# Experts of a mixture-of-experts layer in 13 blocks of mixed pieces instead of 14 of equal ones, a second fixed block, and gathers without empty rows

## What is computed

```python
def _hier_moe(h, w_group, b_group, w_expert, b_expert, w1, w3, w2):
    ...
    g_sel = jnp.argmax(g_logits, axis=-1)
    ...
    top_v, top_i = lax.top_k(e_in, MOE_TOPK)
    gate = (p_g * jax.nn.softmax(top_v, axis=-1)).reshape(-1)
    ids = (g_sel[:, None] * MOE_EXPERTS_PER_GROUP + top_i).reshape(-1)
    ...
        return (jax.nn.silu(xr @ w1[e]) * (xr @ w3[e])) @ w2[e]
```

## Time and profile before

| | |
|---|---|
| median of 3 runs | 2820.74 us |
| the profiled execution | 2825.79 us |
| its span, first to last instruction | 2823.7 us |
| TensorE, VectorE, ScalarE, GpSimd busy | 92%, 56%, 23%, 6% of the span |
| DMA, bytes moved | 618.46 MB, of which expert weights 384 x 1024 KB |
| chain that ended last, by engine | TensorE 12%, DMA 4%, SyncE's queue 1% of the span (as far as it was followed back) |

### The profile page before, as it was taken

One profiled execution on the slowest core, in us unless ns is written; L12 is line 12 of the kernel. 1 busy time (PEld: TensorE's weight loads), 2 busy tenths in 40 slices (PEclk: granted clock), 3 DMA queues, 4 the chain that ended last, 5 costly groups with the idle time before them and its releaser, 6 DMA issues. The chain is left out here.

```text
span 2823.7 us, 34710 instructions
## 1 busy us (share of the span) xinstructions
PE 2608.0 (92%) x12926; PEld 1701.4 (60%) x12926; DVE 1587.3 (56%) x3139; ACT 650.0 (23%) x1415; POOL 158.5 (6%) x179
## 2 busy tenths in 40 slices
PE   6999899999999999979788799999799898899998
PEld 4888788999468888858645233333487544233332
DVE  4887577777578888767534143334544723233334
ACT  4122365565311110012232100000213512000000
POOL 0000222322000000000100000000000000000000
PEclk8999899999999999989999899999999999999999
DMA  8321311110645537623045999999422049999998
GB/s 310 134 83 60 106 35 42 31 33 14 264 146 179 175 131 239 215 99 142 16 180 242 419 419 419 419 420 419 179 83 75 1 198 383 420 419 419 419 419 356
DMA packets 114129, 618.46 MB, mean 219 GB/s; under 512 B 13136, under 2 KB 13728, under 8 KB 64160
## 3 DMA queue, kind: packets, MB, share of 16 engines
q1 hardware_dynamic: 103680, 581.39, 52.3%
q0 software_dynamic: 8832, 30.44, 3.2%
q10 hardware_dynamic: 1440, 4.29, 0.4%
HBM read 606.51 MB, written 9.56 MB: 218 GB/s over the span
## 5 line engine op out<-in xcount | busy, mean ns | idle before, releaser
L3274 PE MATMUL bank<-arena 128*32 128x512 f32 (+2 forms) x2048 | 404.6, 607 | 32.2 <-DMA arena<-in_w 19.4
L530 PE MATMUL bank<-arena 128*128 128x256 f32 x1776 | 414.0, 387 | 21.5 <-ACT arena L498 13.7
L530 PEld LDWEIGHTS bank<-arena 128*128 128x128 f32 x1776 | 340.5, 193 | 92.5 <-issue 34.6
L3274 PEld LDWEIGHTS bank<-arena 128*32 128x32 f32 (+2 forms) x2048 | 133.9, 131 | 277.8 <-issue 266.9
L3302 PE MATMUL bank<-arena 128*32 128x512 f32 (+2 forms) x1024 | 211.7, 640 | 36.8 <-DMA arena<-in_w 34.5
L3316 PE MATMUL bank<-arena 128*128 128x512 f32 x448 | 219.7, 614 | 5.4 <-DVE arena L3437 1.8
L266 PE MATMUL bank<-arena 128*128 128x512 f32 (+1 forms) x608 | 211.6, 503 | 0.9 <-PEq L2713 0.9
L3451 DVE SCALAR_TENSOR_TENSOR arena<-bank,arena 128x512 f32<-128x512 f32 x224 | 168.3, 751 | 73.6 <-PE bank L3316 61.6
L3302 PEld LDWEIGHTS bank<-arena 128*32 128x32 f32 (+2 forms) x1024 | 70.0, 137 | 173.7 <-issue 169.4
L266 PEld LDWEIGHTS bank<-arena 128*128 128x128 f32 x608 | 114.5, 189 | 94.3 <-issue 87.3
L3316 PEld LDWEIGHTS bank<-arena 128*128 128x128 f32 x448 | 71.4, 188 | 151.5 <-DVE arena L3451 90.0
(11 more groups left out here) (500 smaller groups left out, 3900.3 us busy)
## 6 DMA issues: line engine op xcount, KB each, us to landing
arena<-in_w SPq DMA_DIRECT2D x384, 1024.0 KB, 24.7
arena<-in_dense SPq DMA_DIRECT2D x180, 512.0 KB, 4.5
arena<-in_mods SPq DMA_DIRECT2D x128, 512.0 KB, 4.7
arena<-core_rows POOLq DMA_DIRECT2D x48, 256.0 KB, 3.8
arena<-in_xT SPq DMA_DIRECT2D x2, 2048.0 KB, 11.0
token_rows<-arena ACTq DMA_DIRECT2D x8, 512.0 KB, 2.6
arena<-c_row_silu SPq DMA_DIRECT2D x5, 512.0 KB, 4.6
gdn_gate<-arena POOLq DMA_DIRECT2D x8, 256.0 KB, 2.7
```

Source lines behind the costliest of these rows:

```text
L530: mm = pe.matmul(out, w[:, k, :], x[:, k, :], start=(k == 0), stop=(k == K1 - 1))
L3274: mm = pe.matmul(self.bank[2 + t][part, :], xT[i % 2][:, 2 * q + k, part], w[j][:, k, t, :], start=(q == 0 and k == 0), stop=(q == 3 and k ...
```

## The change

The blocks are cut anew: `KINDS` is `ffmmtwttmmmmm`, 13 blocks. `f` is now two blocks, with the experts 28 to 31 (64 rows each); `w` one block of 128; `t` has 96 + 32 rows; `m` 64 + 32 + 32. A lane of 96 rows is two pieces, 64 and 32 columns, with the same weights. The first fixed block is still made by matmuls; the second is gathered, but its experts are known, so SyncE loads its weights ahead of the wait for the order. In layer 1 the early loads are 15 instead of 12; load 15 waits for the transposed norm factor, whose buffer shares its place. A slot without a pair now gets the number 4096, and the gathers leave out rows with numbers over 511; GpSimd clears the two row buffers first. The routing's formulas for a rank's first slot and for its number of rows are new. The spare blocks become 18, still not run.

```diff
-KINDS = "fqpwpqwpwqwppq"
-FIXED = 2
-LANES = {"f": FIXED, "w": 1, "p": 2, "q": 4}
+KINDS = "ffmmtwttmmmmm"
+LANES = {"f": (64, 64), "w": (128,), "t": (96, 32), "m": (64, 32, 32)}
+FIRST_FIXED = NE - FIXED
...
-MOE_EARLY = [12, 12]
+MOE_EARLY = [12, 15]
...
+def pieces_of(kind):
+    at, pieces = 0, []
+    for j, lanes in enumerate(LANES[kind]):
+        while lanes:
+            n = 1 << (lanes.bit_length() - 1)
+            lanes -= n
+            pieces.append((j, slice(at, at + n), lanes == 0))
+            at += n
+    return pieces
...
-            dve.tensor_copy(self.slot_tok, toks).then_inc(s["slots"], 1)
+            dve.tensor_scalar(self.slot_tok, toks, float(NO_ROW), None, ALU.add).then_inc(s["slots"], 1)
...
+                    if n == MOE_RING - 1:
+                        sp.wait_ge(self.rstd_turned, 1)
                     if n >= MOE_RING:
                         sp.wait_ge(s["used"], n - MOE_RING + 1)
...
+                    if i == FIXED_BLOCKS:
                         self.clear_past(sp)
                         sp.wait_ge(self.order_ready, 1)
...
+                for i in range(2):
+                    last = pool.memset(xr[i], 0.0)
+                self.pool.after(pool, last)
                 pool.wait_ge(self.rows_stored, 64)
...
-                    pool.indirect_dma_start(xr[i % 2], None, self.rows[:, :],
-                                            bass.IndirectOffsetOnAxis(at, 0)).then_inc(x_in[i % 2], 16)
+                    pool.indirect_dma_start(xr[i % 2], None, self.rows[:, :], bass.IndirectOffsetOnAxis(at, 0),
+                                            bounds_check=L - 1, oob_is_err=False).then_inc(x_in[i % 2], 16)
...
                         for k in range(2):
                             for t in range(2):
-                                for j, part in enumerate(parts):
+                                for j, part, last in pieces:
                                     mm = pe.matmul(self.bank[2 + t][part, :], xT[i % 2][:, 2 * q + k, part], w[j][:, k, t, :],
                                                    start=(q == 0 and k == 0), stop=(q == 3 and k == 1))
-                                    if k == 1 and t == 1:
+                                    if k == 1 and t == 1 and last:
                                         mm.then_inc(s["used"], 1)
```

More of the change, by code:

```diff
@@ L33 @@
 NG, EG = 4, 8
-KINDS = "fqpwpqwpwqwppq"
-FIXED = 2
-LANES = {"f": FIXED, "w": 1, "p": 2, "q": 4}
-WIDE, PAIRS, QUADS = (KINDS.count(kind) for kind in "wpq")
-HALF, QUARTER = P // 2, P // 4
[L39 to L43, removed]
+KINDS = "ffmmtwttmmmmm"
+LANES = {"f": (64, 64), "w": (128,), "t": (96, 32), "m": (64, 32, 32)}
+COUNT = {kind: KINDS.count(kind) for kind in LANES}
+FIXED_BLOCKS = COUNT["f"]
+FIXED = FIXED_BLOCKS * len(LANES["f"])
+FIRST_FIXED = NE - FIXED
+HALF, QUARTER = P // 2, P // 4
+FIRST_THREE = FIXED + COUNT["w"]
+FIRST_HALF = FIRST_THREE + COUNT["t"]
+BESIDE_THREE = FIRST_HALF + COUNT["m"]
+THIRD = BESIDE_THREE + COUNT["t"]
+FOURTH = THIRD + COUNT["m"]
+assert FOURTH + COUNT["m"] == NE and COUNT["w"] == 1
+FIRST_BLOCK = {"f": 0, "w": FIXED_BLOCKS, "t": FIXED_BLOCKS + 1, "m": FIXED_BLOCKS + 1 + COUNT["t"]}
+MAIN = len(KINDS)
+OVF = 18
 BLOCKS = MAIN + OVF
@@ L128, in constant_tables @@
     e = np.arange(NE)
-    t["bonus"] = np.tile(2048.0 * np.maximum(FIXED - e, 0) - e / 64.0, (P, 1))
+    t["bonus"] = np.tile(2048.0 * np.where(e < FIRST_FIXED, 0, NE - e) - e / 64.0, (P, 1))
     t["fold"] = row % 64 == np.arange(36)[None, :]
@@ L3186, in experts_of @@
                 def experts_of(i):
-                    return list(range(FIXED)) if i == 0 else [expert(r) for r in seq[i][1]]
+                    return [FIRST_FIXED + r for r in seq[i][1]] if i < FIXED_BLOCKS else [expert(r) for r in seq[i][1]]
                 for i in range(N + 1):
@@ L3220, in _ @@
                     sp.wait_ge(s["added"], KD * N)
+                    if layer == 0:
+                        sp.wait_ge(ss, 1)
                     spare_sync(sp)
@@ L3260, in hidden @@
                 def hidden(i, quarters):
-                    parts = seq[i][2]
+                    ranks, pieces = seq[i][1:]
                     if quarters[0] == 0:
@@ L3297, in output @@
                     for t in halves:
-                        w = [slot_in(pe, first2[i] + t * len(parts) + j).rearrange("p (k n) -> p k n", k=4)
-                             for j in range(len(parts))]
+                        w = [slot_in(pe, first2[i] + t * len(ranks) + j).rearrange("p (k n) -> p k n", k=4)
+                             for j in range(len(ranks))]
                         for k in range(4):
-                            for j, part in enumerate(parts):
+                            for j, part, last in pieces:
                                 mm = pe.matmul(self.bank[7 - t][part, :], aT[:, k, part], w[j][:, k, :],
                                                start=(k == 0), stop=(k == 3))
-                                if k == 3:
+                                if k == 3 and last:
                                     mm.then_inc(s["used"], 1)
@@ L3552, in gpsimd_steps @@
         def gpsimd_steps(pool):
+            for i in range(2):
+                pool.memset(xr[i], 0.0).then_inc(cleared, 1)
+            pool.wait_ge(cleared, 2)
             for b in range(B):
```

87 lines of the change are left out of this document (50 added, 37 removed).

## The result

The changed kernel takes 3224.97 us, the median of 4 runs (3222.83 to 3227.96), against 2820.9 us of the kernel before on the same chip: a ratio of 1.1431, 95% interval 1.1413 to 1.1449. The forecast was 2813.3 us. What happened is the second rival, the one with a chance of 0.20: pieces of 64 and of 32 columns don't run at the same time.

The account below looks back on a forecast made before the run. Each layer was taken as bound by DMA bytes after the expert loads' restart, plus what follows the last landing. -2.0 - 5.8 - 5.5 + 3.8 + 2.1 = -7.4 us gave 2813.3 us (-0.26%), range 2801 to 2815, chance 0.47.

Parts of the forecast that it names:

- the second rival: Expert matmuls: 64- and 32-wide pieces don't run at the same time; 15.0 instead of 7.0 us a run, about 3157 us; chance 0.20.
- TensorE inside the stretch: Expert blocks while loads stream: 30.3 us of TensorE against 46.0 of transport if pieces run side by side; costed at nothing.
- Early loads: Expert loads 12 to 15 cross the idle 31 us before the restart; gain 1.0 us a layer, 2.0 in all.
- Gathers: Gathers behind load 28: empty rows left out save their full bytes, 9.8 ns each; -5.8 and -5.5 us.
- Tail: End of each layer: TensorE finishes later after the last landing, as the last block has three experts; +2.1 and +3.8 us.
- The first rival: Whole kernel: nothing measurable, through dearer width changes in the tail (2820.5 us) or empty rows costing as full (2822.1); chance 0.28.
- Costed at nothing: Routing and layer start: two more VectorE instructions (some 1.3 us), two GpSimd memsets and moved semaphore clears delay nothing.

Follow-up runs that it names:

- one-width kernel: The changed kernel with every piece of the ten t and m blocks cut to 32 columns: 2823.49 us, ratio 0.9998 against the kernel before.
- half runs: one-width kernel, each gather leaving out the half of its partitions that one bit names: 2819.5 us (bit 0), 2825.3 (bit 6), 2822.7 for the kernel before.
- edit of the tail: one-width kernel with half scatters done earlier in the last blocks: 2819.63 us, ratio 0.9987 against the kernel before.

## Why the prediction was wrong

**The step that failed.** The term "TensorE inside the stretch" was set to nothing on the condition "if the pieces run side by side". The prediction took it because the changes of width in the trace before are "all between pieces that share columns, so they bind no piece to others' columns". That argument says only that those rows can't show an exclusion; it was read as if they spoke against one. The runs show in its place that a 64 and a 32 on other columns take turns: a run of 15.88 instead of 7.0 us, and back to 7.0 with one width. The Trainium skill, TensorEngine Tiling (Array Packing), section Key Properties, has the rule: changing the tiling mode, and not only the tile, drains the array. By that rule the rival was the forecast, and the trace agrees, with 14.27 us for a run that changes four times and 15.88 for one that changes sixteen times.

**The rival's price.** It had 15.0 us a run and 3157 us in all, against 15.88 and 3225. It took eight pairs of changes at 0.15; a pair costs 0.26 (2.12 / 8). Thirty runs a layer at 0.88 are 26 of the 34 us a layer that it was short; the layer ended at 2205.8 instead of near 2175.

**Early loads.** As forecast in place: load 16 left at 1528.3 (1529 forecast), the 31 us carried 184 instead of 68 GB/s, and load 28 landed 6.5 us after its issue instead of 8.4, in layer 1 7.1 instead of 7.8. That is 1.9 and 0.6 us sooner where 1.0 and 1.0 stood, though with mixed pieces nothing waited for it; in the one-width kernel it was 1.6 and 0.1.

**Gathers: the second step that failed.** The software queue moved 24.74 MB, 5.7 MB less, as forecast. But "the DMA time follows bytes in every row I have, so I take the full saving" was wrong. Of 5.8 and 5.5 us the one-width kernel saved 4.4 in layer 0 (423.1 to 418.7) and lost 0.6 in layer 1 (422.0 to 422.6). In every row before, all partitions were fetched, so bytes and the fullest sixteenth went together; the half runs part them. The fullest group went from 80 rows in ten gathers to 72 in nine in layer 1 and to 68 in layer 0, which by the line above is worth 1.2 and 1.7 us, not 5.5 and 5.8. Runs that should be alike differ by up to 2 us in this measure, so layer 1 fits. That layer 0 saved more than its share stays open, since all three profiles of this layout show it.

**Tail.** The mechanism was right: +2.1 and +3.8 us were forecast, and the one-width kernel's last scatter ends 2.0 and 4.0 us later after the last landing than before. That the size fits so well is luck in part, since two errors cancel. The last block's first quarter started 38.8 us ahead of the last landing, not 37.6; and from there to the end of the first half's scatter TensorE took 42.7 and 43.0 us, not 41.4, because the first output half ran 5.08 and 5.34 us where the forecast had 3.65. The edit of the tail confirms the cause, since 3.1 us of each came back when TensorE's work behind the first quarter's loads was cut.

**The sum without the widths.** -7.4 was forecast, and the one-width kernel gave -0.02% (-0.11% to +0.07%), so 2 us slower to 3 us faster. The gathers in layer 1, 6.1 us short, account for most of the gap. The first rival, no measurable difference, would have been right for this kernel, and by a mechanism that it named, empty rows that cost as much as full ones, though only in layer 1.

**Costed at nothing.** The memsets (1.84 us on GpSimd in the 31 us) and the routing's new instructions delayed nothing: the second fixed block starts at 1560.69, where the quad block started at 1561.59.

## What to carry over

Pieces of a packed matmul should have one column width per stretch of work; in these fp32 runs two widths on disjoint columns take turns, and each change of width costs 0.13 us more. Where a trace can't show a case, it is no evidence against it: a stated rule that names the case, as the one of the Trainium skill cited above did, then deserves the larger chance. When rows are left out of a gather, look at which rows stay: here the time follows the fullest of the sixteen groups of partitions, not the bytes, with one layout that doesn't fit.

## What the runs showed of the hardware

- fp32 matmuls of 64 and 32 columns on disjoint columns take turns (starts at least 0.522 us apart in 955 changes), while two 32s start 6 ns apart. A change of width costs 0.13 us (14.27 and 15.88 us for 4 and 16 changes).
- A row that a gather leaves out still shows as a packet of 4 bytes (9 ns in the trace, against 162 ns for a row of 4096 bytes); a gather of 128 rows with none fetched costs some 0.3 us of transport (3.1 and 2.3 us for the nine gathers behind load 28, the other small losses included), with all fetched some 1.4 (13.4 and 12.4 us).
- Leaving out half of a gather's rows saved 3.8 to 6.2 us a layer by bit 0, 1 or 5 of the partition, and between -1.2 and 0.6 by bit 2, 3 or 6. The trace doesn't say which engine moved a packet. The groups rest on these runs, bit 4 by elimination; that each is one of the 16 DMA engines rests on the section of the Trainium skill named above.
